# Sixteen cache copies inside the gate stage, laid out as many 8 KB rows instead of one or two long ones

## The chip, the cores and the metric

The kernel runs on one core of a Trainium2 chip. The metric is the device time of one execution in microseconds; of several executions the median counts. Engines go by the names of the profile: PE is the matmul engine TensorE, ACT ScalarE, DVE VectorE, POOL GpSimd, SP SyncE. ACTq and SPq are the sequencers of ACT and SP, which also issue DMAs. A core has 16 DMA engines, and all queues share them.

## The reference

One layer of a hybrid decoder, for a prompt of 256 tokens and for 8 decode streams of 4 tokens, all float32, 2048 channels. The part that matters here, shortened:

```python
xn = rmsnorm(x, w['norm_mix_pre'])
z = jnp.einsum('ntd,de->nte', xn, w['w_in'])          # queries, keys, values, gates
...                                                    # four mixer branches: o_a, o_b, o_c, o_d
gates = jax.nn.sigmoid(z[..., OFF_G:].reshape(N, T, N_BRANCH, D_MODEL))
merged = (gates[:, :, 0] * (o_a @ w['p_a']) + gates[:, :, 1] * (o_b @ w['p_b'])
          + gates[:, :, 2] * (o_c @ w['p_c']) + gates[:, :, 3] * (o_d @ w['p_d']))
x = x + rmsnorm(merged @ w['w_o'], w['norm_mix_post'])
f, new['conv'] = conv_ffn(rmsnorm(x, w['norm_ffn_pre']), ...)
...
# sliding caches of the decode streams, one for each of three head groups
new_len = min(win, W + T)
new_buf = jnp.concatenate([buf, jnp.stack([k, v], 2)], 1)[:, W + T - new_len:]
```

The caches hold 128, 512 and 1024 past rows for each of the 8 samples (groups 0, 1 and 2), and a row is 2 x 2 x 128 floats, 2 KB. The outputs have 128, 512 and 1028 rows. So of groups 0 and 1 all but the first four old rows go to the output, of group 2 all 1024, and the four new rows stand behind them. The old rows are copied by DMA from one place in the chip's memory to another; no engine touches them.

## The kernel before

The engines run programs of their own and meet at semaphores. All large matrix products go through **units** of weights: 512 rows by 512 columns, 1 MB. For each unit SP loads w_raw (four buffers), ACT casts it into the high part w_hi (line 704), DVE subtracts to get the low part w_lo (line 1008), and PE does 48 matmuls of 128 x 128 by 288 columns (lines 1492 to 1494: high by high, high by low, low by high). w_hi and w_lo have two buffers each. ACT's cast of unit u waits until the load has landed and until PE has finished unit u - 2. SP's load of unit u waits until DVE has made the low part of unit u - 4, so a load is issued nearly four units before its cast.

The **gate stage** is a loop of four rounds over 512 output channels each. A round has four branches b = 0 to 3, and a branch has five units: four of w_in (the gate columns) and then one of the branch's output matrix, p_a, p_b, p_c or p_d. The unit of p_a is half a unit. Counted through a round, p_a is unit 4, p_b unit 9, p_c unit 14 and p_d unit 19. After the gate columns of a branch ACT takes the sigmoid (line 899), and after it in program order ACT's sequencer issues one copy of old cache rows to an output (line 903), before the cast of unit 5b + 6. A round deals with two samples, and its four copies are:

| branch | cache | samples in the copy | KB |
|---|---|---|---|
| 0 | group 1 | 2 | 2032 |
| 1 | group 2 | 1 | 2048 |
| 2 | group 2 | 1 | 2048 |
| 3 | group 0 | 2 | 496 |

That makes sixteen copies in the stage, 27 MB read and 27 MB written. Only the very end of SP's program waits for them (semaphore copied). The weight loads have no connection with the data of the copies; both use the same DMA engines. The gate stage lies between about 690 and 1280 us of the span. After it come the products with w_o and, from about 1430 us, the channel mixer's units without any such copies.

A copy is written as a slice: for branch 0 the first dimension of both sides is the 2 samples, and behind it stand 508 rows of 2 KB without gaps. For branches 1 and 2 the first dimension has one element, so that one contiguous run of 2 MB is left.

Of the kernel before, what the change touches and what calls it, by code (L numbers as in the profile page):

```python
# [25 lines left out]
NP_TOK, NB, NT = 256, 8, 4  # L26
# [5 lines left out]
WIN_LEN = (128, 512, 1024)  # L32
# [102 lines left out]
def build(nc, known, d, o, ctx):  # L135
    def sem(name):
        return ctx.enter_context(nc.semaphore(name))
# [162 lines left out]
    copied = sem("copied")  # L300
# [33 lines left out]
    def room(k):  # L334

        if k < NA:
            return 3 * (k % 2), 768 * (k % 2), k % 3, 6 * 512
        return (k - NA) % 6, 256 * (k % 3), k % 3, (6 + k % 2) * 512
# [5 lines left out]
    def unit_no(u0, per, i, j):  # L344

        if isinstance(i, int):
            return u0 + per * i + j, (u0 + per * i + j) // N_RAW, j % N_RAW, j % N_SPLIT
        return i * per + (u0 + j), i * (per // N_RAW) + (u0 + j) // N_RAW, j % N_RAW, j % N_SPLIT
# [20 lines left out]
    def _(sp):  # L369
# [15 lines left out]
        def load(no, src):  # L385

            u, _, slot, _ = no
            if not isinstance(u, int) or u >= N_RAW:
                need = u - (N_RAW - 1)
                if not isinstance(need, int):  # L390
                    need = sp.snap(sp.to_reg(need))
                    sp.wait_ge(landed["x"], 16)
                sp.wait_ge(lo_ready, need)
            sp.dma_start(w_raw[slot][:, 0:src.shape[1], 0:src.shape[2]], src).then_inc(w_landed[slot], 16)
# [302 lines left out]
    def _(e):  # L697
        def hi(no, k=SEG, n=UNIT_COLS):

            u, r, slot, s = no  # L700
            e.wait_ge(w_landed[slot], r * 16 + 16)
            if not isinstance(u, int) or u >= N_SPLIT:
                e.wait_ge(unit_done, u - 1)
            e.activation(w_hi[s][:, 0:k, 0:n], w_raw[slot][:, 0:k, 0:n], ACT.Copy).then_inc(hi_ready, 1)  # L704
# [74 lines left out]
        for m in range(3):  # L779
            n = P if m < 2 else NS  # L780
# [34 lines left out]
        for k, (groups, oc, m) in enumerate(units):  # L815
            _, lp, _, at = room(k)
            n = len(groups) * (m + 1) * P
# [73 lines left out]
        with e.Fori(0, 4) as i:  # L891
            for b in range(4):
                for j in range(2, 4):
                    hi(unit_no(U_MIX, 20, i, 5 * b + j))
                hi(unit_no(U_MIX, 20, i, 5 * b + 4), k=P_CHUNKS[b])
                hi(unit_no(U_MIX, 20, i, 5 * b + 5))
                e.wait_ge(unit_done, i * 20 + (U_MIX + 5 * b + 4))
                e.wait_ge(p_used, i * 4 + b)
                e.activation(sig[:, :, :], ps[:, 0:4, 0:TOK], ACT.Sigmoid).then_inc(sig_ready, 1)

                g, n0, nb = ((1, 0, 2), (2, 0, 1), (2, 1, 1), (0, 0, 2))[b]
                first = NT if g < 2 else 0
                e.dma_start(o[9 + g][0, bass.ds(i * 2 + n0, nb), 0:WIN_LEN[g] - first],
                            d[f"cache_win{g}"][0, bass.ds(i * 2 + n0, nb), first:WIN_LEN[g]]).then_inc(copied, 16)
                hi(unit_no(U_MIX, 20, i, 5 * b + 6))
            e.wait_ge(merged_f, i + 1)
            e.activation(M_hi[:, bass.ds(i * 4, 4), :], acc[:, :, :], ACT.Copy).then_inc(merged_hi, 1)
# [9 lines left out]
        for n in range(2, 18):  # L917
            hi(unit_no(U_GATE, 8, 0, n))
            if n % 4 == 1:
                g = n // 4 - 1  # L920
# [73 lines left out]
        for m in range(3):  # L994
            n = P if m < 2 else NS
# [7 lines left out]
    def _(e):  # L1003
        def lo(no, k=SEG, n=UNIT_COLS):

            u, _, slot, s = no
            e.wait_ge(hi_ready, u + 1)
            e.tensor_tensor(w_lo[s][:, 0:k, 0:n], w_raw[slot][:, 0:k, 0:n], w_hi[s][:, 0:k, 0:n].bitcast(F32),  # L1008
                            ALU.subtract).then_inc(lo_ready, 1)
# [158 lines left out]
        def normalise(k):  # L1168
            groups, oc, m = units[k]
            _, lp, c, _ = room(k)  # L1170
            n = len(groups) * (m + 1) * P
            e.wait_ge(act.sem, act.at(("E", k)))
            e.reciprocal(col[:, 6 + c:7 + c], col[:, 3 + c:4 + c]).then_inc(dve.sem, dve.step(("rs", k)))
            e.wait_ge(dve.sem, dve.at(("rs", k)))
            e.tensor_scalar(view(Lp, P, lp, [[1, n]]), view(Lp, P, lp, [[1, n]]), col[:, 6 + c:7 + c], None, ALU.mult)\
                .then_inc(dve.sem, dve.step(("P", k)))
# [773 lines left out]
```

## Time and profile before

| | |
|---|---|
| timed runs (3) | 2316.03, 2316.69, 2318.72 us; median 2316.69 |
| profiled execution | span 2311.6 us from first to last instruction; no other time of it is on record |
| PE / ACT / DVE busy | 91% / 33% / 48% of the span |
| mean granted clock of PE | 0.952 |
| moved by DMA | 377 MB, of it 35.31 MB on ACT's queue q10 |

A busy share tells how full an engine is over the whole kernel, not what the kernel waits for. The chain that ended last and the waits of single instructions tell that, and the order of time shows what happens at one place. The median of the timed runs lies 5.1 us over the profiled span; that part lies before the first and after the last instruction.

### The profile page before, as it was taken

Reading aid. Unit: us, or ns where it says so; the run is one execution under the profiler, and the core shown is the slowest. Engines: PE = TensorE matmul, PEld = TensorE weight load, DVE = VectorE, ACT = ScalarE, POOL = GpSimd, SP = SyncE. Lnnn points to the kernel's source line nnn. Section 1 sums busy time; section 2 is a strip of 40 time slices with the busy share of each in tenths; the row PEclk is TensorE's granted clock in tenths of the full one; section 3 lists DMA queues with packets and bytes.
Section 4 is the critical chain, followed back from the end, with each engine's and each line's share of the span. In section 5 each row is a group of like instructions: output and inputs, shape, how many; then the busy total and the mean of one; then the engine's idle time right before and its main releaser. Section 6 shows DMA issues by size and latency. Waiting matters only on the chain.

```text
span 2311.6 us, 36850 instructions
## 1 busy us (share of the span) xinstructions
PE 2108.5 (91%) x14921; PEld 1934.4 (84%) x14921; DVE 1114.1 (48%) x1108; ACT 773.3 (33%) x643; POOL 81.7 (4%) x172
## 2 busy tenths in 40 slices
PE   7999977899987996987969896999999999999995
PEld 5999965344457996987969895999999999999995
DVE  4333334355542442423424337565556555655564
ACT  3333333233332332323323332433333333333332
POOL 0000011000000000000000001100000000000000
PEclk9999987899989998998989998999999999999998
DMA  6544521677644654546546641555545454455531
GB/s 219 178 163 163 168 75 25 194 201 203 186 154 151 231 177 168 200 154 229 167 176 206 206 164 43 168 168 168 165 163 163 163 163 163 164 166 167 167 117 55
DMA packets 189396, 377.00 MB, mean 163 GB/s; under 512 B 8985, under 2 KB 33841, under 8 KB 188250
## 3 DMA queue, kind: packets, MB, share of 16 engines
q1 hardware_dynamic: 184300, 340.50, 46.0%
q10 hardware_dynamic: 5015, 35.31, 4.1%
q8 instruction: 65, 1.06, 0.2%
q14 instruction: 16, 0.13, 0.0%
HBM read 365.43 MB, written 37.66 MB: 174 GB/s over the span
## 4 chain that ended last, share of the span: by engine, by line
PE 83%; DMA 7%; DVE 5%; ACT 2%; issue 1%; SPq 0%; ACTq 0%; DVEq 0%
PE ps L1492 23%; PE ps L1494 23%; PE ps L1493 23%; DMA w_raw<-in_p_b 7%; PE ps L1474 4%; PE ps L1695 3%; DVE w_lo L1008 1%; PE ps L1480 1%; DVE m_T L1025 1%; PE ps L1798 1%; ACT w_hi L704 1%; PE ps L1799 1%; PE ps L1810 1%; PE ps L1807 1%; PE ps L1813 0%
## 5 line engine op out<-in xcount | busy, mean ns | idle before, releaser
L1008 DVE TENSOR_TENSOR w_lo<-w_raw,w_hi 128x2048 fp32r<-128x2048 f32 (+1 forms) x272 | 614.7, 2260 | 854.9 <-ACT w_hi L704 854.9
L1492 PE MATMUL ps<-xn_hi,w_hi 128*128 128x288 f32 x3104 | 917.0, 295 | 27.5 <-DVE xn_lo L1031 13.8
L1494 PE MATMUL ps<-xn_hi,w_lo 128*128 128x288 f32 x3104 | 918.1, 296 | 0.0
L1493 PE MATMUL ps<-xn_lo,w_hi 128*128 128x288 f32 x3104 | 916.3, 295 | 0.0
L704 ACT ACTIVATE w_hi<-w_raw 128x2048 fp32r<-128x2048 f32 (+1 forms) x272 | 514.3, 1892 | 1128.2 <-PE ps L1494 1009.7
L1492 PEld LDWEIGHTS ps<-xn_hi,w_hi 128*128 128x128 f32 x3104 | 584.6, 188 | 31.9 <-DVE xn_lo L1031 15.4
L1493 PEld LDWEIGHTS ps<-xn_lo,w_hi 128*128 128x128 f32 x3104 | 584.6, 188 | 0.0
L1494 PEld LDWEIGHTS ps<-xn_hi,w_lo 128*128 128x128 f32 x3104 | 584.6, 188 | 0.0
L1492 PE MATMUL ps<-act_hi,w_hi 128*128 128x288 f32 x704 | 207.8, 295 | 2.8 <-DVE act_lo L1393 2.8
L1494 PE MATMUL ps<-act_hi,w_lo 128*128 128x288 f32 x704 | 208.4, 296 | 0.0
L1493 PE MATMUL ps<-act_lo,w_hi 128*128 128x288 f32 x704 | 208.0, 295 | 0.0
L1492 PE MATMUL ps<-O_hi,w_hi 128*128 128x288 f32 x224 | 70.6, 315 | 76.0 <-DVE w_lo L1008 76.0
L1492 PEld LDWEIGHTS ps<-act_hi,w_hi 128*128 128x128 f32 x704 | 132.7, 188 | 3.0 <-DVE act_lo L1393 3.0
L1494 PEld LDWEIGHTS ps<-act_hi,w_lo 128*128 128x128 f32 x704 | 132.8, 189 | 0.0
L1493 PEld LDWEIGHTS ps<-act_lo,w_hi 128*128 128x128 f32 x704 | 132.7, 189 | 0.0
L1492 PEld LDWEIGHTS ps<-O_hi,w_hi 128*128 128x128 f32 x224 | 46.1, 206 | 76.9 <-DVE w_lo L1008 76.9
L1400 DVE TENSOR_TENSOR m_T<-ps,m_T 128x1152 f32<-128x1152 f32 x44 | 59.6, 1355 | 54.9 <-PE ps L1494 54.9
L1377 DVE SCALAR_TENSOR_TENSOR hc<-H,conv,hc 128x304 f32<-128x304 f32 x176 | 82.2, 530 | 0.0
L1492 PE MATMUL ps<-M_hi,w_hi 128*128 128x288 f32 x256 | 76.5, 299 | 6.0 <-DVE w_lo L1008 6.0
L1695 PE MATMUL ps<-kt_b,qs_b 128*16 128x512 f32 x128 | 68.8, 621 | 9.1 <-ACT kt_b L837 6.1
L1494 PE MATMUL ps<-M_hi,w_lo 128*128 128x288 f32 x256 | 76.6, 299 | 0.0
L1493 PE MATMUL ps<-M_lo,w_hi 128*128 128x288 f32 x256 | 76.4, 298 | 0.0
(274 smaller groups left out, 1699.3 us busy)
## 6 DMA issues: line engine op xcount, KB each, us to landing
w_raw<-in_w_in SPq DMA_DIRECT2D x104, 1024.0 KB, 5.1
w_raw<-in_w_up SPq DMA_DIRECT2D x88, 1024.0 KB, 5.0
w_raw<-in_w_down SPq DMA_DIRECT2D x44, 1024.0 KB, 5.1
kv<-in_cache_k SPq DMA_DIRECT2D x64, 256.0 KB, 2.9
kv<-in_cache_v SPq DMA_DIRECT2D x64, 256.0 KB, 2.9
w_raw<-in_w_o SPq DMA_DIRECT2D x16, 1024.0 KB, 5.1
kv<-in_cache_win SPq DMA_DIRECT2D x16, 512.0 KB, 6.4
out<-in_cache_win ACTq DMA_DIRECT2D x4, 2032.0 KB
```

The lines of the kernel that those rows point to most:

```text
L704: e.activation(w_hi[s][:, 0:k, 0:n], w_raw[slot][:, 0:k, 0:n], ACT.Copy).then_inc(hi_ready, 1)
L1008: e.tensor_tensor(w_lo[s][:, 0:k, 0:n], w_raw[slot][:, 0:k, 0:n], w_hi[s][:, 0:k, 0:n].bitcast(F32), ALU.subtract).then_inc(lo_ready, 1)
L1025: e.scalar_tensor_tensor(out=dst[:, c, :], in0=src[:, c, :], scalar=gains[:, g + c:g + c + 1], in1=stat[:, 2, :], op0=ALU.mult, op1=ALU.mult)\
L1377: e.scalar_tensor_tensor(out=dst, in0=src, scalar=w[tap], in1=dst, op0=ALU.mult, op1=ALU.add)\
L1400: e.tensor_tensor(m_T[:, 4 * j:4 * j + 4, :], ps[:, 4 * (j % 2):4 * (j % 2) + 4, 0:TOK], m_T[:, 4 * j:4 * j + 4, :], ALU.add).then_inc(y_a ...
L1474: return e.transpose(dst, src, ident[0:n, 0:n])
L1480: mm = e.matmul(ps[:, bank, 0:TOK], ones[:, :], sq[:, q, k, :], start=q == 0 and k == 0, stop=q == 3 and k == 3)
L1492: e.matmul(dst, w_hi[s][:, r, cols], x_hi[:, k0 + r, :], start=first and r == 0, stop=False)
L1493: e.matmul(dst, w_hi[s][:, r, cols], x_lo[:, k0 + r, :], start=False, stop=False)
L1494: mm = e.matmul(dst, w_lo[s][:, r, cols], x_hi[:, k0 + r, :], start=False, stop=last and r == k - 1)
L1695: e.matmul(ps[0:16, 4 + half, :], qs_b[:, 16 * h:16 * h + 16], kt_b[:, q % 2, :], start=h == 0, stop=h == 3).then_inc(scored, 1)
L1798: e.matmul(ps[0:32, 3, :], pt_b[0:k, pg, :], hi_v, start=pg == 0, stop=False, skip_group_check=True)
```

## The change

```diff
                 g, n0, nb = ((1, 0, 2), (2, 0, 1), (2, 1, 1), (0, 0, 2))[b]
-                first = NT if g < 2 else 0
-                e.dma_start(o[9 + g][0, bass.ds(i * 2 + n0, nb), 0:WIN_LEN[g] - first],
-                            d[f"cache_win{g}"][0, bass.ds(i * 2 + n0, nb), first:WIN_LEN[g]]).then_inc(copied, 16)
+                first = NT * 512 if g < 2 else 0
+                size = WIN_LEN[g] * 512 - first
+
+                def flat(a, at):
+                    a = a.rearrange("l n r v h e -> (l n) (r v h e)")
+                    return a[bass.ds(i * 2 + n0, nb), at:at + size].rearrange("a (p x) -> p a x", p=(32, 128, 256)[g])
+                e.dma_start(flat(o[9 + g], 0), flat(d[f"cache_win{g}"], first)).then_inc(copied, 16)
                 hi(unit_no(U_MIX, 20, i, 5 * b + 6))
```

The same bytes are copied at the same place of ACT's program, with the same semaphore. Each sample's old rows are taken as one flat run of floats, which is cut into p equal rows, and the order of the dimensions is then rows, samples, floats in a row. For group 1 that is 128 rows by 2 samples by 2032 floats (8128 bytes), for group 2 256 rows by 1 sample by 2048 floats (8192 bytes), for group 0 32 rows by 2 samples by 1984 floats (7936 bytes).

## Rows read from the trace of the kernel before

**Rows 1.** The page: chain that ended last by line; costliest groups.

```profile
PE ps L1492 23%; PE ps L1494 23%; PE ps L1493 23%; DMA w_raw<-in_p_b 7%; PE ps L1474 4%; PE ps L1695 3%; DVE w_lo L1008 1%; PE ps L1480 1%; DVE m_T L1025 1%; PE ps L1798 1%; ACT w_hi L704 1%; PE ps L1799 1%; PE ps L1810 1%; PE ps L1807 1%; PE ps L1813 0%
...
L1008 DVE TENSOR_TENSOR w_lo<-w_raw,w_hi 128x2048 fp32r<-128x2048 f32 (+1 forms) x272 | 614.7, 2260 | 854.9 <-ACT w_hi L704 854.9
```

**Rows 2.** The table of waits: who waited for what, total us, times, longest.

```profile
ACT w_hi L704 <- DMA w_raw<-in_p_b: 101.9, 4, 25.6
```

**Rows 3.** ACT in order of time, third round: start, us, engine, line, operation [idle before].

```profile
1003.59 0.67 ACTq L903 DMA_DIRECT2D out<-in_cache_win  x1
...
1020.74 1.92 ACT L704 ACTIVATE w_hi<-w_raw 128x2048 fp32r<-128x2048 f32 x1 [4.44 <-PE ps L1494]
...
1048.04 1.91 ACT L704 ACTIVATE w_hi<-w_raw 128x2048 fp32r<-128x2048 f32 x1 [25.38 <-DMA w_raw<-in_p_b]
...
1068.10 1.92 ACT L704 ACTIVATE w_hi<-w_raw 128x2048 fp32r<-128x2048 f32 x1 [4.44 <-PE ps L1494]
...
1087.18 1.92 ACT L704 ACTIVATE w_hi<-w_raw 128x2048 fp32r<-128x2048 f32 x1 [4.44 <-PE ps L1494]
...
1087.52 0.55 ACTq L903 DMA_DIRECT2D out<-in_cache_win  x1
...
1093.54 1.92 ACT L704 ACTIVATE w_hi<-w_raw 128x2048 fp32r<-128x2048 f32 x1 [3.42 <-PE ps L1494]
```

**Rows 4.** Busy time by stretch: us, PE, PEld, DVE, ACT, POOL, clock, DMA share, GB/s.

```profile
1027.00:1048.00 21.00, 6.42 (x49) 6.19 (x47) 0.00 (x0) 0.00 (x0) 0.00 (x0) 0.76 0.21 81
1048.00:1062.00 14.00, 9.67 (x52) 9.67 (x53) 4.75 (x3) 5.09 (x4) 0.00 (x0) 0.63 0.77 272
1430.00:1600.00 170.00, 170.00 (x1285) 170.00 (x1285) 99.54 (x101) 64.36 (x46) 14.77 (x29) 1.00 0.49 162
```

**Rows 5.** SP's queue in order of time: start, us of the issue.

```profile
1007.62 0.37 SPq L394 DMA_DIRECT2D w_raw<-in_p_b  x1
...
1091.57 0.37 SPq L394 DMA_DIRECT2D w_raw<-in_p_d  x1
```

**Rows 6.** The page: DMA issues, with KB each and median us to landing.

```profile
w_raw<-in_w_in SPq DMA_DIRECT2D x104, 1024.0 KB, 5.1
...
w_raw<-in_p_b SPq DMA_DIRECT2D x4, 1024.0 KB, 40.4
w_raw<-in_p_c SPq DMA_DIRECT2D x4, 1024.0 KB, 12.2
w_raw<-in_p_d SPq DMA_DIRECT2D x4, 1024.0 KB, 8.2
```

**Rows 7.** DMA queues in 1024 to 1044: packets, MB, share of 16 engines.

```profile
q10 hardware_dynamic: 16, 1.04, 12.0%
q1 hardware_dynamic: 16, 0.03, 0.4%
```

**Rows 8.** DMA queues in 1087 to 1119.

```profile
q10 hardware_dynamic: 48, 2.10, 17.2%
```

**Rows 9.** DMA queues in 2290 to 2311, where y_nat is stored in 8192-byte rows.

```profile
q1 hardware_dynamic: 336, 2.36, 29.7%
```

**Rows 10.** ACT in order of time: the last cast before and fourth after each hole.

```profile
723.80 1.92 ACT L704 ACTIVATE w_hi<-w_raw 128x2048 fp32r<-128x2048 f32 x1 [4.44 <-PE ps L1494]
...
771.30 1.92 ACT L704 ACTIVATE w_hi<-w_raw 128x2048 fp32r<-128x2048 f32 x1 [4.44 <-PE ps L1494]
...
872.88 1.92 ACT L704 ACTIVATE w_hi<-w_raw 128x2048 fp32r<-128x2048 f32 x1 [4.44 <-PE ps L1494]
...
919.18 1.92 ACT L704 ACTIVATE w_hi<-w_raw 128x2048 fp32r<-128x2048 f32 x1 [4.44 <-PE ps L1494]
...
1169.68 1.92 ACT L704 ACTIVATE w_hi<-w_raw 128x2048 fp32r<-128x2048 f32 x1 [4.44 <-PE ps L1494]
...
1216.16 1.92 ACT L704 ACTIVATE w_hi<-w_raw 128x2048 fp32r<-128x2048 f32 x1 [4.44 <-PE ps L1494]
```

**Rows 11.** The issues at line 903: ns min/median/max, first and last start.

```profile
L903 ACTq DMA_DIRECT2D out<-in_cache_win x16: 541/643/837, 706.7 to 1267.3; - x16
```

## The prediction

> **What bounds the kernel now.** I read the page first. Its chain that ended last is TensorE almost throughout, with one foreign body: 7% of the span is a load of the third kind of weight block, w_raw<-in_p_b [rows 1]. Seven per cent of 2311.6 us is 162 us, and there are four such loads, so the chain runs through about 40 us of each of them. The table of waits says the same from the other end: ScalarE's cast L704 waited four times for that load, 101.9 us together [rows 2]. No other weight matrix stands in either view with such a number. So TensorE sets the end except at four places, and the question is what holds one load in twenty of the gate stage.
>
> ScalarE's own order of time gives the picture [rows 3]. One unit of weights costs TensorE 6.36 us (1087.18 to 1093.54 is one step; 170 us for 1285 matmuls in a later stretch is 0.132 us each, times 48 is 6.35 us [rows 4]). The cast at 1020.74 should be followed by one at 1027.10. It came at 1048.04, after 25.38 us of waiting for in_p_b. In that hole TensorE worked 6.42 of 21 us, and when it came back its granted clock averaged 0.63 over the next 14 us, a mixture of the 2.4 and the 1.2 GHz level, where the long stretch afterwards has 1.00 [rows 4]. The price of a hole is therefore the wait and a slow restart.
>
> **Why the load is late.** The copy of branch 0 was issued at 1003.59 [rows 3], the in_p_b load at 1007.62 [rows 5], and the load landed 40.4 us later, where ordinary loads of the same 1024 KB need 5.1 us [rows 6]. In the middle of this time, 1024 to 1044, the queues show 16 pieces of the copy's queue, 1.04 MB, and 16 pieces of the loads' queue, 0.03 MB, and the copy's share is 12.0% of sixteen engines [rows 7]. Two of sixteen engines are 12.5%: the copy sits on two engines. A piece is 1.04 MB/16 = 65 KB and takes 0.120 x 16 x 20/16 = 2.4 us, so an engine moves 27 GB/s. One small piece of the load passes for each large piece of the copy; the other fourteen engines are empty. Each of the two engines has 2.08/2 = 1.04 MB of copy and 0.07 MB of the load: 1.11 MB/27 GB/s = 41 us, which from 1003.6 gives 1045, against 1048.0 observed. The arithmetic leaves little for any other cause.
>
> The copies of branches 1 and 2 move just as much, but as one contiguous run. In 1087 to 1119 such a copy is 48 packets, 2.10 MB, 17.2% of sixteen engines over 32 us [rows 8]: 88 engine-us, 5.5 us on each of sixteen. The loads behind those two copies landed in 12.2 (in_p_c) and 8.2 us (in_p_d) [rows 6], and no step of 6.36 us was lost there [rows 3].
>
> **The change, part by part.**
> Copy 0 (two samples, 2.08 MB). The old form has 2 as its outermost count, the new one 128 rows of 8128 bytes, with the samples inside. That this spreads it over all engines I take from the loads, whose outermost count is 128 also: 1024 KB in 5.1 us is 206 GB/s [rows 6], four times what two engines gave (1.04 MB in 20 us, 52 GB/s) [rows 7]. The Trainium skill (DMA: Bandwidth & Descriptors, "Why a DMA increments its semaphore by 16 and not by 1") says that the number of engines is the largest one up to 16 that divides the slowest dimension of both sides, which would be 2 before and 16 after; rows 7 agree for the 2, and no row here shows the 16 for this shape. Each engine then has 16 pieces. Price of a piece from two sides: 8128 bytes at 27 GB/s is 0.30 us; the stores of 8192 bytes at the kernel's end took 0.297 x 16 x 21/288 = 0.35 us each (2.36 MB are 288 of them) [rows 9]. So 4.8 to 5.5 us an engine; I take 5.5, the contiguous copy's figure too.
>
> When does in_p_b land then? The nearest case is copy 2 with in_p_d: copy at 1087.52, load at 1091.57, 4.05 us later [rows 3, 5], landed in 8.2 us. Here the distance is 1007.62 - 1003.59 = 4.03 us. From above: the whole copy still in front, 5.1 + 5.5 = 10.6, or in_p_c's 12.2. The load is due at 1027.10, 19.5 us after its issue. Even 12.2 leaves 7.3 us. The wait goes completely, and what is late next is nothing: the cast waits for TensorE again.
>
> What that gives is read from four holes, as the time over four casts less 4 x 6.36 = 25.44 us [rows 3, 10]: 771.30 - 723.80 = 47.50, loss 22.06; 919.18 - 872.88 = 46.30, loss 20.86; 1068.10 - 1020.74 = 47.36, loss 21.92; 1216.16 - 1169.68 = 46.48, loss 21.04. The slow restart lies inside these differences. Sum: 85.9 us.
>
> Copies 1 and 2 (2.10 MB each): 32 pieces of 64 KB (with a closing packet on each of sixteen engines the 48 of [rows 8]) become 256 of 8 KB, on sixteen engines before and after; 16 x 0.30 to 0.35 = 4.8 to 5.6 us an engine against 5.5. Their loads had landings of 8.2 and 12.2 us and are due some 21 us after issue (four steps of 6.36 less the 4.2 us of cast and low part that the issue waits for). Cost 0; without cover it would be a few tenths of a us each. Copy 3 (0.51 MB): from two engines with 0.25 MB each, 9.4 us at 27 GB/s, to four pieces an engine, 1.4 us. Nothing waits for it now, gain 0. The final wait for all copies lies a thousand us later.
>
> Issue on ScalarE's queue: 16 issues, 0.54 to 0.84 us now, median 0.64 [rows 11]. The new ones have 64 to 256 pieces instead of 8 to 32; a load of 512 pieces needs 0.37 us on SyncE's queue [rows 5]. Bounds 0.37 and, where the number of pieces should count, twice the present greatest, 1.7; I take 0.64 unchanged. Behind it in ScalarE's order stands the next cast; it has 3.42 us of idle before it [rows 3], and behind that 6.36 - 1.92 - 2.26 = 2.2 us before TensorE misses the low part [rows 1, 3]. Also 1.7 us is covered. Uncovered it would be 16 us at most. SyncE issues nothing new; its loads are only no longer held back.
>
> **Sum.** Span 2311.6 - 85.9 = 2225.7. The median of the runs lies 5.1 us over the profiled span, so 2316.7 - 85.9 = 2230.8 us.
>
> **Rivals.**
> *A rest of the wait stays.* Small pieces from and to the same memory may be slower than large ones. The copy may hold an engine for 19.5 - 5.1 + 4.0 = 18.4 us before in_p_b is late, 1.15 us a piece against 0.30 to 0.35. If copying ran at a quarter of the 381 GB/s that rows 8 give (2.10 MB/5.5 us), so 95 GB/s, copy 0 would need 21.9 us: 3.5 us late, four times, 14 us; copies 1 and 2 have 20.1 us of room (21.2 - 5.1 + 4.0), 2 us late each, 16 us. That gives 2261; half the rate gives 11 us and no wait. Against it: 88 engine-us for 2.10 MB [rows 8] come to 0.34 us per 8192 bytes for a memory-to-memory copy, and [rows 9] to 0.35 for small rows that are only written. The Trainium skill (DMA: Bandwidth & Descriptors, "Latency and other measured facts") has memory-to-memory copies at 207 GB/s in rows of a 512 KiB pitch and 103 at 4 MiB; by its 207 the sum stays, by its 103 (20 us for each large copy) it would be some 2240. The pitch here is 8 KB. Chance 0.05, most of it with only a few us left over.
>
> *The change doesn't do what it says.* If the form were merged back or the samples stayed outermost, copy 0 would keep two engines, in_p_b its 40.4 us, and the time would be 2316.7. For it speaks only that no row shows this form; 128 rows with 2 inside can't be joined into one run. Chance 0.04.
>
> *Slower: the pieces clog all engines.* Now only two engines are blocked, and only one load in twenty is late. If an 8 KB piece cost c us, each of the three large copies would hold every engine for 16c, with room of 18.4, 20.1 and 20.1 us: the loss per round is 48c - 59. It equals today's 21.5 at c = 1.68 us, five times the price of rows 9. At c = 2.4, where a piece had a fixed cost of today's large one, the loss is 56 us a round, and the time 2231 + 225 = 2456. Against it: 2 KB pieces of the loads pass at 206 GB/s over sixteen engines, 0.16 us each at most. Chance 0.02.
>
> **How the numbers follow.** Full removal has 0.89. Its own range: four times the least hole (20.86) or the greatest (22.06) is 83.4 to 88.2 us, 2228.5 to 2233.3, and with the spread of the runs before (0.7 below, 2.0 above the median) 2228 to 2235. For issue costs that show through (up to some 3 us) and a gain at copy 3 that I count at nothing I go to 2226 and 2238, which also takes in the mild part of the first rival. Less than 2 in 10 is left out. Faster by over 0.2% (4.6 us, about what a measurement of this kernel can tell from no change) 0.94, within it 0.04, slower 0.02.
>
> **What would show it.** In the profile after: no wait of L704 for in_p_b, and no DMA in the chain; in_p_b landing in 8 to 12 us; 272 packets for copy 0, about 9% of sixteen engines over some 60 us instead of 12% in a row; steps of 6.36 us through the whole stage; clock 1.00 where it was 0.63. Wrong would be: in_p_b over 19.5 us; a cast waiting for in_p_c or in_p_d; an issue at L903 over 5 us; or a granted clock under 1.00 in the stage without a hole before it.

## The result and the profile after

Four timed runs of the changed kernel have a median of 2231.8 us (2230.12 to 2234.92), four of the kernel before 2317.0 us (2316.03 to 2318.72). The ratio is 0.9632, 95% interval 0.9616 to 0.9647: 85 us faster. Forecast were 2230.8 us and a range of 2226 to 2238.

The profiled execution has a span of 2231.0 us and took 2232.71 us itself, so 1.7 us lie outside the span. In every execution whose span and time are both on record it is 1.7 to 1.8 us.

The page's chain that ended last, by line (1496 to 1498 are the matmuls that were 1492 to 1494; the change put four lines in front of them):

```profile
PE ps L1496 25%; PE ps L1498 25%; PE ps L1497 25%; PE ps L1478 4%; PE ps L1699 3%; PE ps L1484 1%; DVE m_T L1029 1%; PE ps L1802 1%; PE ps L1803 1%; PE ps L1814 1%; PE ps L1811 1%; PE ps L1817 0%; PE ps L1755 0%; PE ps L1647 0%; DVE w_lo L1012 0%
```

The 7% of in_p_b of [rows 1] are gone from the chain, and no wait of L704 for a weight load is left in the table of waits, against [rows 2]. ScalarE in order of time, third round again:

```profile
965.90 0.61 ACTq L908 DMA_DIRECT2D out<-in_cache_win  x1
...
983.05 1.92 ACT L704 ACTIVATE w_hi<-w_raw 128x2048 fp32r<-128x2048 f32 x1 [4.44 <-PE ps L1498]
...
989.41 1.92 ACT L704 ACTIVATE w_hi<-w_raw 128x2048 fp32r<-128x2048 f32 x1 [4.44 <-PE ps L1498]
...
1008.49 1.92 ACT L704 ACTIVATE w_hi<-w_raw 128x2048 fp32r<-128x2048 f32 x1 [4.44 <-PE ps L1498]
...
1027.89 0.54 ACTq L908 DMA_DIRECT2D out<-in_cache_win  x1
```

Copy 0 is issued at 965.90, and the cast of in_p_b's unit runs at 989.41, one step of 6.36 us behind the one at 983.05. The fourth cast after 983.05 is at 1008.49, 25.44 us later, where [rows 3] has 47.36. The same casts of the first and the fourth round (in [rows 10] the first and the last row):

```profile
728.67 1.92 ACT L704 ACTIVATE w_hi<-w_raw 128x2048 fp32r<-128x2048 f32 x1 [4.44 <-PE ps L1498]
...
1135.62 1.92 ACT L704 ACTIVATE w_hi<-w_raw 128x2048 fp32r<-128x2048 f32 x1 [4.44 <-PE ps L1498]
```

Between them lie 406.95 us, before 492.36: the stage has become 85.4 us shorter. TensorE in the whole stage, from the first to the last issue of a copy (stretch, its length, PE, PEld, DVE, ACT, POOL, clock, DMA share, GB/s):

```profile
711.00:1187.00 476.00, 466.73 (x3511) 465.14 (x3511) 206.83 (x104) 169.48 (x101) 0.00 (x0) 1.00 0.64 218
```

The clock is 1.00 over 476 us; [rows 4] had 0.63 after a hole. The DMA issues, with KB each and median us to landing:

```profile
w_raw<-in_p_b SPq DMA_DIRECT2D x4, 1024.0 KB, 7.3
w_raw<-in_p_c SPq DMA_DIRECT2D x4, 1024.0 KB, 7.7
w_raw<-in_p_d SPq DMA_DIRECT2D x4, 1024.0 KB, 8.3
```

In_p_b lands in 7.3 us instead of 40.4, in_p_c in 7.7 instead of 12.2 [rows 6]. What in_p_c had before it in the kernel before was not copy 0, whose last data piece had passed by 1044, but what the hole left behind. SyncE's queue in the third round before:

```profile
1025.20 19.65 SPq L394 DMA_DIRECT2D w_raw<-in_w_in  x1
...
1052.49 0.37 SPq L394 DMA_DIRECT2D w_raw<-in_w_in  x1
1055.09 3.80 SPq L394 DMA_DIRECT2D w_raw<-in_p_c  x1
```

Two loads of w_in that had been issued before the hole, at 1011.95 and 1018.84, landed only after it, at 1050.6 and 1053.1; a third was held in its issue until 1044.85, the fourth was issued at 1052.49, and copy 1 had been issued at 1051.00. In_p_c came behind all of these. In the changed kernel copy 1 stands just as far ahead of it (996.09 and 1000.18), but there is no such crowd of loads.

The queues in the ten microseconds around copy 0, 964 to 974 (packets, MB, share of 16 engines):

```profile
q10 hardware_dynamic: 272, 2.08, 58.8%
q1 hardware_dynamic: 529, 1.05, 28.1%
```

This answers to [rows 7]. All 2.08 MB pass within ten microseconds, at 58.8% of sixteen engines and not at 12.0%: 256 pieces and one closing packet on each of sixteen engines. A piece costs 0.588 x 16 x 10/256 = 0.37 us, an engine's sixteen 5.9 us. For copy 1, in 995 to 1027, the queue shows:

```profile
q10 hardware_dynamic: 48, 2.10, 17.0%
```

That is the row of [rows 8] over again, 48 packets. Rows of a single sample follow each other without a gap and come out as one run again, in pieces of 64 KB; the new layout has changed nothing for copies 1 and 2. The issues on ScalarE's queue (ns min/median/max) are as long as in [rows 11]:

```profile
L908 ACTq DMA_DIRECT2D out<-in_cache_win x16: 541/598/759, 711.5 to 1186.8; - x16
```

### The profile page after: what moved, and what is told of

Its sections match the earlier page's. It is cut to its first block, busy times and chain, and to the rows that moved or that the text cites. A ratio compares the mean times of both kernels' runs of the same rounds, so it can differ in the third digit from the quotient of the medians.

```text
span 2231.0 us, 36850 instructions
## 1 busy us (share of the span) xinstructions
PE 2099.9 (94%) x14921; PEld 1927.0 (86%) x14921; DVE 1114.5 (50%) x1108; ACT 773.4 (35%) x643; POOL 81.9 (4%) x172
## 4 chain that ended last, share of the span: by engine, by line
PE 90%; DVE 5%; ACT 2%; issue 1%; ACTq 1%; SPq 1%; DMA 0%; DVEq 0%
PE ps L1496 25%; PE ps L1498 25%; PE ps L1497 25%; PE ps L1478 4%; PE ps L1699 3%; PE ps L1484 1%; DVE m_T L1029 1%; PE ps L1802 1%; PE ps L1803 1%; PE ps L1814 1%; PE ps L1811 1%; PE ps L1817 0%; PE ps L1755 0%; PE ps L1647 0%; DVE w_lo L1012 0%
## 5 line engine op out<-in xcount | busy, mean ns | idle before, releaser
L1496 PE MATMUL ps<-xn_hi,w_hi 128*128 128x288 f32 x3104 | 917.8, 296 | 28.0 <-DVE xn_lo L1035 13.8
L704 ACT ACTIVATE w_hi<-w_raw 128x2048 fp32r<-128x2048 f32 (+1 forms) x272 | 514.4, 1892 | 1042.5 <-PE ps L1498 1028.9
L1478 PEld LDWEIGHTS ps<-ident,kv 128*128 128x128 f32 (+1 forms) x384 | 41.1, 147 | 38.2 <-ACT kt_b L837 20.0
L1498 PE MATMUL ps<-O_hi,w_lo 128*128 128x288 f32 x224 | 66.1, 295 | 0.0
```

The source lines that it names most:

```text
L1478: return e.transpose(dst, src, ident[0:n, 0:n])
L1496: e.matmul(dst, w_hi[s][:, r, cols], x_hi[:, k0 + r, :], start=first and r == 0, stop=False)
L1498: mm = e.matmul(dst, w_lo[s][:, r, cols], x_hi[:, k0 + r, :], start=False, stop=last and r == k - 1)
```

## The experiments

All times are medians in us. The stage is the time from the first to the last issue of a copy in the profiled execution, which leaves out everything ahead of the change: the first issue itself comes anywhere between 706.7 and 715.2 in these profiles. "in_p_b" is its median time from issue to landing; 19.5 us are allowed. That column alone doesn't tell what a run lost: in runs 4, 6 and 12 in_p_b was in time and the loads behind it were not (in_p_c landed in 26.4, 47.3 and 21.2 us).

| run | copy 0 | time | before, same chip | ratio, 95% interval | in_p_b | stage |
|---|---|---|---|---|---|---|
| before | 2 engines, 65 KB | | 2317.0 | | 40.4 | 560.6 |
| changed | 16, 8 KB | 2231.8 | 2317.0 | 0.9616 to 0.9647 | 7.3 | 475.3 |
| 1 copy 0 alone | 16, 8 KB | 2229.9 | 2314.5 | 0.9612 to 0.9651 | 7.8 | 475.2 |
| 2 copy 3 alone | 2, 65 KB | 2316.1 | 2314.5 | 0.9991 to 1.0011 | 40.2 | 560.9 |
| 3 one sample each | 16, 65 KB | 2231.9 | 2314.5 | 0.9620 to 0.9652 | 7.4 | 474.9 |
| 4 two engines | 2, 8 KB | 2299.3 | 2314.5 | 0.9924 to 0.9957 | 16.9 | 543.3 |
| 5 four engines | 4, 65 KB | 2234.2 | 2316.4 | 0.9627 to 0.9666 | 21.3 | 476.7 |
| 6 127 rows | 1, 8 KB | 2417.4 | 2316.4 | 1.0421 to 1.0461 | 17.2 | 662.3 |
| 7 16 rows | 16, 65 KB | 2230.7 | 2316.4 | 0.9618 to 0.9655 | 7.4 | 475.9 |
| 8 2048 rows | 16, 0.5 KB | 2230.7 | 2316.4 | 0.9615 to 0.9664 | 17.0 | 476.1 |
| 9 no copies | none | 2232.3 | 2314.8 | 0.9636 to 0.9666 | 5.1 | |
| 10 changed again | 16, 8 KB | 2229.1 | 2314.8 | 0.9623 to 0.9650 | 7.5 | 475.8 |
| 11 state_conv later | 16, 8 KB | 2223.7 | 2314.8 | 0.9594 to 0.9620 | 7.5 | 475.6 |
| 12 254 rows | 2, 4 KB | 2250.7 | 2314.7 | 0.9702 to 0.9738 | 12.1 | 495.6 |

**Theories.** A: copy 0's outermost count of 2 puts it on two of sixteen engines; on those, load and copy take turns piece by piece, so a load of 32 small pieces needs as long as 32 turns or the rest of the copy; the change spreads the copy and nothing else matters. B: the other copies bring part of the gain. C: it is the size of the pieces that lets the load through, not the number of engines.

**Runs 1 and 2: one copy alone.**

```diff
+                if g == 1:
+                    first = NT * 512 if g < 2 else 0
...
+                    e.dma_start(flat(o[9 + g], 0), flat(d[f"cache_win{g}"], first)).then_inc(copied, 16)
+                else:
+                    first = NT if g < 2 else 0
+                    e.dma_start(o[9 + g][0, bass.ds(i * 2 + n0, nb), 0:WIN_LEN[g] - first],
+                                d[f"cache_win{g}"][0, bass.ds(i * 2 + n0, nb), first:WIN_LEN[g]]).then_inc(copied, 16)
```

The lines left out are those of the change. Run 2 has g == 0 in the first line.

> Only the copy of branch 0 (two samples of group 1, 2.08 MB) has the new form; the other three of a round keep the old slices. Theory A (the gain is copy 0's spread over all sixteen engines, which frees the in_p_b load): 2232 us, within 3 us of the changed kernel, with in_p_b landing in 7 to 9 us and in_p_a back at 9.4 us, because copy 3 stays on two engines. Rival B (the other copies' form brings part of the gain): more than 5 us above 2232.

> Only the copy of branch 3 (two samples of group 0, 0.51 MB) has the new form. Theory A: no change, 2317 us within 4, in_p_b landing 40 us; in_p_a landing falls from 9.4 to about 4 us and nothing waits for it. Rival B: at least 5 us faster than before.

Copy 0 alone gives the whole gain (stage 475.2 us), copy 3 alone none. The issues of run 2:

```profile
w_raw<-in_p_b SPq DMA_DIRECT2D x4, 1024.0 KB, 40.2
...
w_raw<-in_p_a SPq DMA_DIRECT2D x4, 512.0 KB, 3.8
```

Copy 3's form does what was to be expected for its own neighbour, in_p_a lands in 3.8 us and not in about 9.3 as in run 1, but no one had waited for it. B falls.

**Run 3: two DMAs of the old form, one sample each.**

```diff
+                if g == 1:
+                    for n in range(2):
+                        first = NT if g < 2 else 0
+                        e.dma_start(o[9 + g][0, bass.ds(i * 2 + n, 1), 0:WIN_LEN[g] - first],
+                                    d[f"cache_win{g}"][0, bass.ds(i * 2 + n, 1), first:WIN_LEN[g]]).then_inc(copied, 16)
+                else:
...
```

The other three copies have the new form here, and SP waits for twenty copies at its end instead of sixteen; the latter holds for runs 4 and 5 too.

> Copy 0 is issued as two DMAs of the old slice form, one sample each (a contiguous run of 1.04 MB), so that the pieces stay as large as before (about 65 KB) and one issue is added in each round. Theory A (number of engines decides, not the size of the pieces): 2232 us within 4, in_p_b landing in 7 to 11 us. Rival C (the smaller pieces of the new form are what lets the load through): 2300 to 2317 us, in_p_b landing near 40 us.

```profile
out<-in_cache_win ACTq DMA_DIRECT2D x8, 1016.0 KB, 6.9
...
w_raw<-in_p_b SPq DMA_DIRECT2D x4, 1024.0 KB, 7.4
```

The pieces are as large as before, and the wait is gone all the same. C falls as a necessary condition: large pieces over sixteen engines do.

**Run 7: 16 rows of 65024 bytes a sample, in one DMA.**

```diff
-                    return a[bass.ds(i * 2 + n0, nb), at:at + size].rearrange("a (p x) -> p a x", p=(32, 128, 256)[g])
+                    return a[bass.ds(i * 2 + n0, nb), at:at + size].rearrange("a (p x) -> p a x", p=(32, 16, 256)[g])
```

> Copy 0 as in the changed kernel, but in 16 rows of 65024 bytes for each sample: sixteen engines with two large pieces each, in one DMA. Theory A: 2232 us within 3, in_p_b landing in 7 to 10 us. Rival C (small pieces are needed): in_p_b later than 19.5 us and a wait for it.

Same result in one DMA: 2230.7 us, in_p_b in 7.4 us. The copy's queue in 962 to 972, ten microseconds around copy 0 as above:

```profile
q10 hardware_dynamic: 48, 2.08, 59.6%
```

That is 0.596 x 16 x 10/32 = 3.0 us for 65 KB, 22 GB/s an engine, the rate of the 8 KB pieces.

**Run 4: two engines, but small pieces.**

```diff
+                    if n is not None:
+                        return a[bass.ds(i * 2 + n, 1), at:at + size].rearrange("a (p r x) -> (a r) p x", r=2, x=2032)
...
+                for n in range(2) if g == 1 else (None,):
+                    e.dma_start(flat(o[9 + g], 0, n), flat(d[f"cache_win{g}"], first, n)).then_inc(copied, 16)
```

> Copy 0 as two DMAs, one sample each, with outermost count 2 and 64 rows of 8128 bytes inside (every second row, so that rows can't be joined): meant to have two engines, but small pieces. Theory A1 (on these two engines one piece of the copy passes for each piece of a load, whatever its size): each load has 32 pieces on an engine and is held by 32 x 0.30 = 9.6 us, so in_p_b lands in 13 to 17 us and is in time, but loads then come every 12 us against a need of 6.36, and the third and fourth after it are some 5 and 10 us late: 10 to 12 us lost a round, 2270 us (2255 to 2290). Theory A2 (a load waits for all bytes of the copy in front of it on an engine): 2317 us, in_p_b at 40 us. Rival C (only the size of the pieces counts): 2232 us.

It took 2299.3 us, between the theories and above the range of A1. ScalarE in order of time in the second round:

```profile
875.76 1.92 ACT L704 ACTIVATE w_hi<-w_raw 128x2048 fp32r<-128x2048 f32 x1 [4.44 <-PE ps L1501]
...
886.17 1.92 ACT L704 ACTIVATE w_hi<-w_raw 128x2048 fp32r<-128x2048 f32 x1 [8.49 <-DMA w_raw<-in_w_in]
...
899.95 1.91 ACT L704 ACTIVATE w_hi<-w_raw 128x2048 fp32r<-128x2048 f32 x1 [10.85 <-DMA w_raw<-in_w_in]
...
911.76 1.92 ACT L704 ACTIVATE w_hi<-w_raw 128x2048 fp32r<-128x2048 f32 x1 [9.91 <-DMA w_raw<-in_w_in]
...
924.24 1.92 ACT L704 ACTIVATE w_hi<-w_raw 128x2048 fp32r<-128x2048 f32 x1 [7.94 <-PE ps L1501]
```

In_p_b is in time, as A1 had it. The next three loads (w_in) are late, and come 13.8 and 11.8 us apart. The copy's queue in 866 to 882:

```profile
q10 hardware_dynamic: 84, 0.67, 10.1%
```

A piece takes 0.101 x 16 x 16/84 = 0.31 us, 26 GB/s. Eighty-four pieces in 16 us on two engines are one in 0.38 us on each, the load's piece beside it included, and 32 of these turns are 12.2 us, as A1 had it. So the mechanism is A1's, taking turns, and my sum was too small: from 875.76 to 924.24 are 48.48 us for five steps of 6.36, 16.7 us lost a round and not 10 to 12. I had reckoned with in_p_b at the early end of its range and let the second load behind it still be in time; at 16.9 us already the first is late (8.49 us of idle against 4.44), and the next two come 7.4 and 5.4 us later still against the need. In the 13.8 us copy 1, issued at 886.50, is on the engines too. TensorE's slow restart comes on top, at a share that I didn't separate. 4 x 16.7 = 67 us on 2232 makes 2299. A2 (all bytes ahead of the load) and C (piece size alone) are both refuted: on a crowded engine both the number of engines and the size of a piece count.

**Run 5: four engines, large pieces.** As run 4, with this line in place of run 4's:

```diff
+                        return a[bass.ds(i * 2 + n, 1), at:at + size].rearrange("a (p r x) -> (a r) p x", r=4, x=16256)
```

> Copy 0 as two DMAs, one sample each, with outermost count 4 and 4 rows of 65024 bytes inside: meant to have four engines and today's large pieces. Theory A: 8 pieces of 2.4 us an engine, 19.2 us from about 1 us after the first issue, so in_p_b lands in 18 to 21 us where 19.5 are allowed: 0 to 3 us lost a round, 2232 to 2244 us. Rival (the number of engines is not set by the outermost count): 2232 us with in_p_b at 8 us, or 2317 with 40.

The copy's queue in 842 to 858, and ScalarE's casts behind it:

```profile
q10 hardware_dynamic: 28, 1.56, 23.4%
```

```profile
855.49 1.92 ACT L704 ACTIVATE w_hi<-w_raw 128x2048 fp32r<-128x2048 f32 x1 [4.44 <-PE ps L1501]
863.50 1.91 ACT L704 ACTIVATE w_hi<-w_raw 128x2048 fp32r<-128x2048 f32 x1 [6.10 <-DMA w_raw<-in_p_b]
868.21 1.92 ACT L704 ACTIVATE w_hi<-w_raw 128x2048 fp32r<-128x2048 f32 x1 [2.79 <-PE ps L1501]
```

23.4% of sixteen engines stands for four (25%), as 12.0% stood for two. In_p_b lands in 21.3 us, 1.8 over what is allowed, and the cast comes 8.01 us behind the last instead of 6.36. The stage grows by only 1.4 us in all: 1.65 us are less than the 2.2 us of cover between ScalarE's cast and TensorE. Landings much beyond 19.5 + 2.2 = 21.7 us should show in the time, by this estimate.

**Run 6: 127 rows of 8192 bytes instead of 128 of 8128.**

```diff
-                    return a[bass.ds(i * 2 + n0, nb), at:at + size].rearrange("a (p x) -> p a x", p=(32, 128, 256)[g])
+                    return a[bass.ds(i * 2 + n0, nb), at:at + size].rearrange("a (p x) -> p a x", p=(32, 127, 256)[g])
```

> Copy 0 as in the changed kernel, but cut into 127 rows of 8192 bytes instead of 128 of 8128. Theory A with the rule of the Trainium skill (DMA: Bandwidth & Descriptors, Why a DMA increments its semaphore by 16 and not by 1: the largest number up to 16 that divides the slowest dimension): one engine, 254 pieces of 0.30 us, 76 us and more with the loads between. That engine then has 76 + 12 us of copies and 51 us of loads for a round of 119 us: 2340 to 2400 us, slower than the kernel before. Rival (rows are dealt out over the engines in blocks, whatever their number): 8 rows on each of fifteen engines and 7 on one, 2232 us.

One row fewer makes the kernel 4.4% slower than before the change, and 187 us slower than run 7 on the same chip. The copy's queue in 898 to 910:

```profile
q10 hardware_dynamic: 31, 0.25, 5.0%
```

5.0% is less than one engine's 6.25%, with the loads taking the rest of it. The time is 17 us over my range, and the table of waits and the order of time name what I had left out:

```profile
ACT w_hi L704 <- issue: 145.1, 5, 35.0
...
ACT w_hi L704 <- DMA w_raw<-in_w_in: 116.0, 16, 13.2
```

```profile
917.69 1.92 ACT L704 ACTIVATE w_hi<-w_raw 128x2048 fp32r<-128x2048 f32 x1 [8.48 <-DMA w_raw<-in_w_in]
918.02 34.96 ACTq L908 DMA_DIRECT2D out<-in_cache_win  x1
919.51 1.11 ACT L899 ACTIVATE sig<-ps 128x1152 f32<-128x1152 f32 x1
953.10 3.71 ACT L704 ACTIVATE w_hi<-w_raw 128x2048 fp32r<-128x2048 f32 x2 [32.48 <-issue]
```

The issue of copy 1 at 918.02 took 34.96 us. ScalarE's sequencer is held in it, and the next cast waits 32.48 us for the issue, not for data. What was still in line can be counted. From copy 0's issue to 918 its queue moved 85 of the 254 pieces, so 169 were left on the one engine; from 884 to 953, when the issue came free, it moved

```profile
q10 hardware_dynamic: 177, 1.45, 5.1%
```

so 77 were left. The copy-1 issues of all four rounds took 34.96 to 37.44 us. In_p_b landed in 17.2 us, in time; but a load's 32 turns take 12.4 us (an estimate, at 0.39 us a turn) against a need of 6.36, so the loads behind it fell back further, in_p_c to 47.3.

**Run 12: 254 rows of 4096 bytes.**

```diff
-                    return a[bass.ds(i * 2 + n0, nb), at:at + size].rearrange("a (p x) -> p a x", p=(32, 128, 256)[g])
+                    return a[bass.ds(i * 2 + n0, nb), at:at + size].rearrange("a (p x) -> p a x", p=(32, 254, 256)[g])
```

> Copy 0 as in the changed kernel, but cut into 254 rows of 4096 bytes for each sample. By the divisor rule (254 is 2 x 127) that is two engines with 254 pieces each. Theory A1 (one piece of the copy passes for each piece of a load): a load is held by 32 x 0.16 = 5 us, so loads come every 7.7 us against a need of 6.36 and in_p_b lands in 10 to 13 us; 0 to 3 us lost a round, 2232 to 2245 us. Theory A3, after the run with 2048 rows, where in_p_b landed in 17.0 us and not under 10 (small pieces pass several at a time, so that a load is held as by 8 KB pieces): in_p_b in 16 to 18 us and about 2299 us, as with two engines and 8128 bytes. Rival (254 rows are dealt over all engines): 2232 us, in_p_b under 9 us, and more than 20% of sixteen engines for the copy's queue in the 25 us behind its issue.

```profile
q10 hardware_dynamic: 86, 0.35, 8.6%
```

This is 860 to 870: 86 pieces in 10 us on two engines are a turn of 0.233 us, 32 turns 7.4 us (expected: 7.7). In_p_b lands in 12.1 us, in A1's range and not in A3's or the rival's. So 254 rows are two engines, 127 one, 128 sixteen, and 4 four. The Trainium skill (DMA: Bandwidth & Descriptors, "Why a DMA increments its semaphore by 16 and not by 1") says that a DMA takes the largest number of engines up to 16 that divides the slowest dimension of both sides. These four runs agree with it; for their counts the largest power of two up to 16 would be the same number, and no run has a count, such as 12 or 100, that tells the two rules apart. The time, 2250.7 us, is 6 above A1's range. Its cause is again an issue:

```profile
L908 ACTq DMA_DIRECT2D out<-in_cache_win x16: 541/672/11872, 713.6 to 1209.2; - x16
```

The longest is 11.9 us, and copy 1's issue was held in all four rounds (10.1 to 11.9 us). The casts behind them waited 34.6 us together, some 21 more than the 3.4 us each that they wait anyway, and the stage grew by 20.3. In the second round copy 1's issue started at 877.45 and took 10.10 us. Copy 0's queue had moved 259 of 508 pieces by then and 345 when it came free, so each of the two engines had some 125 pieces left at the start and 81 at the end. That is nearly the number of run 6, although the turns differ by a factor of 1.7. In run 4, where by the same count (171 of 256 moved) some 43 of 128 were left, the longest issue was 0.83 us.

**Run 8: 2048 rows of 508 bytes.**

```diff
-                    return a[bass.ds(i * 2 + n0, nb), at:at + size].rearrange("a (p x) -> p a x", p=(32, 128, 256)[g])
+                    return a[bass.ds(i * 2 + n0, nb), at:at + size].rearrange("a (p x) -> p a x", p=(32, 2048, 256)[g])
```

> Copy 0 in 2048 rows of 508 bytes for each sample: 4096 pieces, 256 an engine. Theory A: bytes alone would be 5 us an engine; with a fixed cost of up to 0.1 us a piece 26 us; in_p_b shares one piece for one and lands within 10 us, so the load stays in time and the time is 2232 to 2240 us if the issue stays under 5 us. The rival side of the prediction: the issue at ScalarE grows with the pieces (the eight state_conv issues with 1408 pieces take 7.4 us, so 4096 pieces would be 21 us), which is about 15 us over its cover, four times, 2290 us.

The kernel is as fast as with 128 rows, and the issue is not longer (0.54 to 0.76 us): the rival of a growing issue falls. But in_p_b took 17.0 us, not under 10. The copy's queue in 715 to 719, five to nine us behind the issue:

```profile
q10 hardware_dynamic: 844, 0.43, 125.4%
```

These are 0.43 MB in 4 us, 107 GB/s over all engines, where the 64 KB pieces of [rows 8] come to 381 by their share; a piece costs 1.254 x 16 x 4/844 = 0.095 us (the share is over 100%, so pieces overlap). The loads' queue has no packet at all in these four us, though in_p_b had been issued at 714.06. Turns of one for one don't explain that, and run 12 shows such turns for 4 KB pieces. From 727 to 731 this run has them too, 581 pieces of the loads' queue and 578 of the copy's; what held the load for its first 8 us stays open. 2.5 us of the 19.5 were left.

**Runs 9 and 10: no copies, and the changed kernel again.** Run 9 leaves out the sixteen copies and the wait for them.

> The sixteen copies and the final wait for them are left out, so the old rows of the three decode caches are missing from the outputs. Theory A: in the changed kernel the copies lie wholly under TensorE's work, so this is 2231 us, within 3 of the changed kernel. Rival: some cost of the copies is left (issues, contention): more than 5 us below it.

> The changed kernel itself, as a base for the next run on the same chip: 2232 us within 3.

```profile
708.00:1184.00 476.00, 466.68 (x3511) 465.09 (x3510) 206.85 (x104) 169.28 (x101) 0.00 (x0) 1.00 0.48 162
```

This row of run 9 covers the same part of the program as the stage's row of the changed kernel above: PE busy for 466.68 of 476 us, against 466.73 with the copies. ScalarE's casts that begin and end it stand at 708.36 and 1183.75, 475.39 us apart, against 475.34 (711.16 and 1186.50) with the copies. 2232.3 against 2229.1 us on the same chip lie in each other's spread (2229.75 to 2236.54 and 2228.49 to 2232.87). What the copies cost now is less than these runs can tell.

**Run 11: the issues behind the stage.** The trace after showed another place where ScalarE's queue is held: eight loads of state_conv, issued in a row between two casts.

```diff
-        for c in range(8):
...
-            e.dma_start(crow[16 * c:16 * c + 16, :, :], ...).then_inc(landed["crow"], 16)
         for n in range(2, 18):
             hi(unit_no(U_GATE, 8, 0, n))
+            if 6 <= n < 14:
+                c = n - 6
...
+                e.dma_start(crow[16 * c:16 * c + 16, :, :], ...).then_inc(landed["crow"], 16)
```

> The changed kernel, and the eight state_conv issues after the gate stage are no longer in a row on ScalarE's queue ahead of the next cast, but one behind each of the casts 6 to 13 of the following loop. In the changed kernel they take 7.4 us (1199.7 to 1207.2), TensorE stands for 6 us and restarts at a granted clock of 0.50 to 0.65 for about 6 us. If the issues are what holds it: 6 to 9 us less, 2223 to 2226 us. Rival: the hole is the large reload of x or the handover between the stages: no change, 2232 us.

The order of time of run 10, and the windows 1195 to 1215 of run 10 and of run 11:

```profile
1195.66 7.69 ACTq L918 DMA_DIRECT2D crow<-in_state_conv  x8
1203.46 3.71 ACT L704 ACTIVATE w_hi<-w_raw 128x2048 fp32r<-128x2048 f32 x2 [10.42 <-issue]
1216.56 1.92 ACT L704 ACTIVATE w_hi<-w_raw 128x2048 fp32r<-128x2048 f32 x1 [9.39 <-PE ps L1498]
```

```profile
1195.00:1215.00 20.00, 13.75 (x89) 13.52 (x88) 4.71 (x3) 3.71 (x2) 0.00 (x0) 0.83 1.04 303
```

```profile
1195.00:1215.00 20.00, 20.00 (x153) 20.00 (x153) 9.47 (x5) 6.18 (x4) 0.00 (x0) 1.00 0.73 276
```

TensorE is busy in all of the 20 us, at full clock, instead of 13.75 at 0.83. 2223.7 against 2229.1 us, intervals of the ratios 0.9594 to 0.9620 and 0.9623 to 0.9650: 5 us faster. From the last copy's issue to the end of the span it is 1036.9 against 1043.9 us, 7.0 less, within the 6 to 9 expected; the medians differ by less, 5.3 us, and in these two profiles the first copy of run 11 comes 2.5 us later, ahead of anything that was changed. It is the fastest version here, 91 us under the kernel before on the same chip.

## Why the prediction was right, point by point

- **What bounds the kernel.** Four holes behind in_p_b, TensorE elsewhere: runs 1 and 2 show it, and without the holes nothing else surfaced in the stage.
- **Why the load is late.** Two engines, 12.0% for 12.5%: shown by the series 1, 2, 4 and 16 engines (5.0, 12.0, 23.4 and 58.8% of the sixteen, loads beside them) and by their times.
- **Landing after.** Forecast 8.2 from the nearest case and at most 12.2, measured 7.3, a little under the 8 to 12 that were named as the sign. The near case carried. The bound of 12.2 was read from in_p_c, whose load stood behind the crowd that the hole had left; that made it too high, on the safe side.
- **Price of a piece.** Forecast 0.30 to 0.35 us, measured 0.37, 22 GB/s an engine. It goes with the number of engines at work and not with the size of the piece: with two of them it was 27 GB/s for 65 KB [rows 7] and 26 for 8 KB (run 4), with sixteen 22 to 24 for 65 KB (run 7; copy 1) and 22 for 8 KB. An engine was held for 5.9 us where 18.4 were allowed.
- **Sum of the holes.** 85.9 us forecast, 85.4 measured between the same casts.
- **From the span to the time.** The term that was mis-described: I put 5.1 us outside the span, being the median less the profiled span. Measured are 1.7 us outside it, here and in every other run. So the profiled execution of before was some 3.4 us faster than the median of the runs. And the new span is 2231.0, 80.6 us less and not 85.9, because its first copy was issued 4.8 us later (711.5 against 706.7), ahead of everything that the change touches. Since a difference was subtracted from a median, the error did not reach the time; the forecast of the span, 2225.7, was off by 5.3 us.
- **Copies 1 and 2.** The step that failed without consequence: I let them become 256 pieces each and gave the merging back a chance of 0.04 for copy 0. They were merged back, 48 packets as before. The cost of 0 was right for a reason other than mine.
- **Issues.** Unchanged, 0.60 for 0.64 us in the median. The bound of 1.7 us that I set on their growth was no bound: where over some 80 pieces of the copy before were still in line on an engine (runs 6 and 12), the next issue took 10 to 37 us, not for its own pieces but for those. (A copy of 256 pieces an engine, run 8, was issued in 0.76 us with nothing in line.) The kernel before had this hold on SyncE's queue, 19.65 us for the load issued at 1025.20. The prediction counted no term for it and needed none, since the cast of that load's unit waited for TensorE (4.44 us, the row at 1068.10 in [rows 3]); in the profile after no issue of a weight load takes over 2.2 us. In the changed kernel a copy lands in 8.7 us and has long left the queue when the next is issued.
- **The other side.** I looked for it in a price of 1.68 us a piece. Run 6 shows where it lies: in a row count that leaves one engine.

## What to carry to other kernels

When one load in a stream lands several times later than its like, look at what another queue was issued just ahead of it and divide that queue's share by one engine's 6.25%: if it comes out as one, two or four, the layout's outermost count is the first suspect, and a count that is a multiple of sixteen (16, 128 and 2048 here) or one contiguous run is what to try. A background copy must be costed on the engines that it really uses, and with the time for which it holds the next issue, of its own queue and of the queue whose pieces pile up behind it. Subtract a stage's gain from the median, and compare stages between fixed instructions, since spans of single executions differ by some microseconds for other reasons.

## What the runs showed of the hardware that was not expected

- A DMA issue can hold its sequencer for tens of microseconds: 34.96 us in run 6 and 10.10 us in run 12, in the rounds counted until 77 and 81 pieces of the earlier copy were left on an engine, and 0.83 us at most in run 4 with some 43 left. It also happens to a queue that is only the victim: in the kernel before SyncE's issue at 1025.20 took 19.65 us, with pieces of three loads in line behind copy 0 on two engines, and it ended at 1044.85, when copy 0 was through. Whether a number of pieces is what counts, and which, no run varied by itself.
- Two engines copying give 26 to 27 GB/s each, with pieces of 65 KB (2.4 us) and of 8 KB (0.31 us); sixteen at once, beside the loads, give 22 to 24, again with both sizes (2.7 to 3.0 and 0.37 us).
- Pieces of 508 bytes move at about 107 GB/s over all engines, and a load issued 4 us behind 4096 of them had no piece through between 1 and 8 us after its own issue and landed in 17.0 us.
